# Handing out PSUM banks by age instead of by turn, from the attention stage to the third branch

## What is computed

```python
z = x @ w_in_2                                   # one wide projection, cut into parts
# branch 1: differential attention, 4 heads, causal, with a position bias
a  = softmax(q1 k1^T * d**-0.5 - slope*dist) - lam * softmax(q2 k2^T * d**-0.5 - slope*dist)
oa = rms_norm(a @ v)
# branches 2 and 3: gated linear attention, state S_t = diag(exp(g_t)) S_{t-1} + k_t^T v_t
ob = rms_norm(q_t S_t) * silu(gout)              # 4 heads of 64x128, two heads to a job
oc = rms_norm(q_t S_t) * silu(hout)              # 4 heads of 128x128, one head to a job
# mixing
y   = einsum('btnc,ncd->btnd', [oa, ob, oc], w_branch)
mix = einsum('btnd,btnd->btd', sigmoid(mg), y) @ w_out_2
```

## Time and profile before

| | |
|---|---|
| median of 3 runs | 2969.69 us |
| profiled execution, its own time | 2970.0 us |
| its span, first to last instruction | 2968.0 us |
| TensorE (PE) busy | 2869.4 us, 97% |
| VectorE (DVE) busy | 1823.4 us, 61% |
| ScalarE (ACT) busy | 1134.8 us, 38% |
| GpSimd (POOL) busy | 1373.5 us, 46% |
| mean granted TensorE clock | 0.993 |
| stretch from the attention stage to the third branch | about 1117 to 2054 us of the span |
| mixing stage (`pe_branches`) | 2054 to 2228 us |

### The profile page before, as it was taken

How to read it: one execution, slowest core, us unless ns; L and a number is a source line. 1 busy time by engine, 2 the same in 40 slices (tenths; PEclk the granted TensorE clock), 3 DMA queues, 4 the chain that set the end, 5 groups by cost and what they waited for, 6 DMA issues and landing times.

```text
span 2968.0 us, 36400 instructions
## 1 busy us (share of the span) xinstructions
PE 2869.4 (97%) x14022; PEld 2361.3 (80%) x14022; DVE 1823.4 (61%) x2849; ACT 1134.8 (38%) x1649; POOL 1373.5 (46%) x697
## 2 busy tenths in 40 slices
PE   8999999999989999999999999999999999999998
PEld 7777778888878877777777887888888788888886
DVE  8837675555458775554647755652354756657886
ACT  4223354444433334344434533432231543433331
POOL 4434348977758662111211111111222599847874
PEclk9999999999999999999999999999999999999999
DMA  6342302333244321111101111124322144463441
GB/s 218 83 124 75 107 15 89 108 106 107 96 170 171 106 87 65 56 58 57 43 29 51 50 57 38 49 71 149 135 100 107 36 146 156 156 216 128 149 149 71
DMA packets 114301, 295.79 MB, mean 100 GB/s; under 512 B 14545, under 2 KB 23169, under 8 KB 114113
## 3 DMA queue, kind: packets, MB, share of 16 engines
q1 hardware_dynamic: 114128, 293.46, 29.8%
HBM read 216.61 MB, written 76.81 MB: 99 GB/s over the span
## 4 chain that ended last, share of the span: by engine, by line
PE 87%; DVE 4%; ACT 3%; POOL 3%; issue 3%; DMA 1%; SPq 0%; ACTq 0%; DVEq 0%; POOLq 0%
PE PS L493 28%; PE PS L926 23%; PE PS L1085 4%; PE PS L1083 4%; PE PS L1084 4%; PE PS L1332 3%; PE PS L533 2%; PE PS L535 2%; PE PS L534 2%; PE PS L1208 1%; POOL WL L3151 1%; PE PS L1238 1%; PE PS L559 1%; PE PS L1105 1%; PE PS L1104 1%
## 5 line engine op out<-in xcount | busy, mean ns | idle before, releaser
L3151 POOL TENSOR_TENSOR WL<-WR,WH 128x1024 fp32r<-128x1024 f32 x236 | 580.1, 2462 | 1212.2 <-ACT WH L1453 1212.0
L1453 ACT ACTIVATE WH<-WR 128x1024 fp32r<-128x1024 f32 x237 | 248.6, 1054 | 279.2 <-POOL WR L3191 137.1
L493 PE MATMUL PS<-XH,WH 128*128 128x512 f32 x1040 | 338.8, 407 | 16.2 <-DVE XL L2213 9.1
L493 PE MATMUL PS<-XL,WH 128*128 128x512 f32 x1040 | 323.0, 392 | 0.0
L493 PE MATMUL PS<-XH,WL 128*128 128x512 f32 x1040 | 321.9, 391 | 0.0
L926 PE MATMUL PS<-XH,WH 128*128 128x512 f32 x624 | 244.1, 391 | 1.6 <-ACT PC L1753 1.6
L926 PE MATMUL PS<-XL,WH 128*128 128x512 f32 x624 | 243.3, 390 | 0.0
L926 PE MATMUL PS<-XH,WL 128*128 128x512 f32 x624 | 243.2, 390 | 0.0
L2735 DVE TENSOR_TENSOR XF<-XF,PS 128x512 f32<-128x512 f32 x280 | 186.8, 682 | 77.7 <-PE PS L1085 77.5
L493 PEld LDWEIGHTS PS<-XH,WH 128*128 128x128 f32 x1040 | 183.1, 189 | 63.2 <-issue 25.1
L493 PEld LDWEIGHTS PS<-XH,WL 128*128 128x128 f32 x1040 | 195.8, 188 | 42.9
(11 more groups left out here) (407 smaller groups left out, 6119.2 us busy)
## 6 DMA issues: line engine op xcount, KB each, us to landing
WR<-in_weights SPq DMA_DIRECT2D x201, 512.0 KB, 3.6
HR<-hsum SPq DMA_DIRECT2D x70, 512.0 KB, 3.7
hsum<-CT SPq DMA_DIRECT2D x40, 512.0 KB, 3.1
DW<-in_weights SPq DMA_DIRECT2D x40, 512.0 KB, 5.4
hsum<-CT SPq DMA_DIRECT2D x40, 256.0 KB, 2.4
gates<-EG SPq DMA_DIRECT2D x18, 512.0 KB, 5.2
EI<-gates SPq DMA_DIRECT2D x18, 512.0 KB, 5.2
hbuf<-CT SPq DMA_DIRECT2D x14, 512.0 KB, 3.0
```

What stands on the lines that cost most here:

```text
L493: last = e.matmul(PS[:, u.b + h, :], w, x[:, k, 512 * h:512 * h + 512], start=k == 0 and w is w1 and x is xh, stop=k == nk - 1 and w is w2)
L1453: e.activation(WH[:, v % NSPL, :], raw_at(r), ACT.Copy).then_inc(w_hi, 1)
L3151: e.tensor_tensor(WL[:, v % NSPL, :], raw_at(r), WH[:, v % NSPL, :].bitcast(F), ALU.subtract).then_inc(w_lo, 1)
```

## The change

`Banks` gets a flag `oldest_first`, a count of events, and for each bank the number of its last event. An event is a `take` or a `let`. With the flag set, `take` without a fixed bank picks, of the banks or pairs with nothing held, the one whose last event is longest ago; of a pair the younger bank counts. The flag is set after the three opening features of the attention stage and cleared after the mixing stage, where `turn` is set to the oldest pair. Nothing else differs: neither the order of instructions on any engine, nor the data that they move, apart from the bank numbers and the semaphores that go with them.

```diff
+        self.oldest_first, self.uses, self.last_use = False, 0, [0] * 8
+
+    def mark(self, b, n):
+        self.uses += 1
+        for x in range(b, b + n):
+            self.last_use[x] = self.uses
+
+    def oldest(self, n):
+
+        free = [b for b in range(0, 8, n) if not any(x in self.held for x in range(b, b + n))]
+        return min(free, key=lambda b: max(self.last_use[b:b + n]))
 
     def take(self, name, n=1, hold=False, told=True, at=None):
-        b = -(-self.turn // n) * n % 8 if at is None else at
-        while any(x in self.held for x in range(b, b + n)):
-            b = (b + n) % 8
-        if at is None:
-            self.turn = b + n
+        if at is None and self.oldest_first:
+            b = self.oldest(n)
+        else:
+            b = -(-self.turn // n) * n % 8 if at is None else at
+            while any(x in self.held for x in range(b, b + n)):
+                b = (b + n) % 8
+            if at is None:
+                self.turn = b + n
+        self.mark(b, n)
...
     def let(self, u):
         for x in range(u.b, u.b + u.n):
             self.held.discard(x)
+        self.mark(u.b, u.n)
...
             pe_open(e, [(("dq", 0), "w_in_2", 0), (("dk", 0), "w_in_2", 512), ((("dv", 0), "x"), "w_in_2", 1024)])
+            bk.oldest_first = True
             fill = iter(())
...
             pe_branches(e)
+            bk.oldest_first = False
+            bk.turn = bk.oldest(2)
             pe_project_out(e, "x3", "w_out_2", range(4), lambda j: [(m_lo, 2 * j + 2)])
```

## The result

| | before | after |
|---|---|---|
| median of 4 runs | 2969.7 us (2967.0 to 2973.18) | 2948.45 us (2946.78 to 2948.72) |
| ratio, 95% interval | | 0.9924 [0.9911, 0.9936] |
| profiled execution, its own time | 2970.0 us | 2948.72 us |
| its span | 2968.0 us | 2946.7 us |
| mean granted clock | 0.993 | 0.992 |

The kernel is 21.25 us faster; 2950.2 (2946.0 to 2957.5) was forecast. The page after shows work of the same size. GpSimd stands before its weight cuts for 20.4 us less, as PE's slots come free that much earlier. Source lines have moved: L493 is now L509, L559 is L575, L1208 is L1224, L1221 is L1237, L1332 is L1349, L1342 is L1359, L1359 is L1376, L1382 is L1399, L2805 is L2824, L3006 is L3025, L3151 is L3170.

A forecast was written before the change was run, and what follows sets the result against it. PE, busy 97%, was taken as the bound. Gains of 16.5 + 2.7 + 1.2 less 0.85 made 19.5 us off the profiled 2970.0, so 2950.5; 0.3 lower for the median, 2950.2 us. Range 2946 to 2957.5.

The forecast's parts named there:

- The whole waits: Between 1117 and 2054 us, 16 PE waits for undrained banks vanish: 16.5 us idle, plus 2.7 us of overlaps.
- the overlap of 0.17: Without a wait, the next matmul starts 0.17 us before the modelled end of the last; each whole wait returns this.
- Waits in part: Two waits before five transposes, behind a values readout, move to the turning of VX: gain 1.2 us, not 2.3.
- New waits: Three places get a bank drained late: scores of step 28, second output lots of jobs 0 and 1; 0.85 us lost.
- Job 1: Level scores behind LG: PE gains 0.7 and DVE comes forward with it; gain taken whole, 0.9 kept for the range.
- The clock: The clock dip behind two waits in job 3, costing some 1.7 us, stays: one dip before and one after.
- the clock rival: Dips in the stretch change: the one goes, 2948.5 us (chance 0.06), or jobs 2 and 4 get it too, 2953.6 (0.05).
- Behind the stretch: After 2054 us the mixing stage and the rest keep their banks and only start earlier; loss put at nothing.
- the opening of the mixing stage: The branch operand stored and loaded again from job 5's last output transposes starts from PE; loss put at nothing.
- runs into the next engine: PE comes early but waits longer for DVE or ACT; 10.0 us lost up to job 1's levels, 2960; chance 0.10.
- slower: Attention steps of 5 to 8 key blocks: PE waits for an AT copy before each score lot; 26 us, 2976; chance 0.03.
- no effect: The waits have a second cause behind the bank, such as weights or operands; 2967 us; chance 0.04.

The follow-up runs named there:

- the tested kernel: Full change with GpSimd's low parts of weight units 180 and 181, cut in job 1, made on 8 of 1024 columns only; one run, 2945.84 us.
- the two halves: Against before: age rule in the attention stage alone, 2965.18 us (ratio 0.9978); age rule in gated and mixing stages alone, 2954.68 us (0.9943).

## Why the prediction was right, and where it was wrong

- **The whole waits: right.** 19.01 measured against 19.2, all sixteen. What carried it was to ask at each wait which lot had the new bank and when that was drained. The putting back of three gates shows cause and size by itself.
- **The cost of one wait: 0.1 too small.** To the idle time and the overlap of 0.17 comes a slower second matmul. It shows at some of the sixteen (0.10 or 0.11 before four projection steps, 0.08 before level scores, nothing before the scores of the attention), 0.8 us in all.
- **Waits in part: right.** 1.08 against 1.2, with L575 <- VX at 11 waits and 10.5 us as said.
- **New waits: right in place, a little high in size.** Measured 0.37 (AT), 0.12 and 0.46 (the two output lots), less what PE caught up: 0.57 against 0.85.
- **Job 1: the step that failed.** I wrote that L3006 at 1593.24 (2.89) stood for ACT's exponentials, that PE leads this chain, and so took the gain of 0.7 whole. In truth it stood beside a weight cut of GpSimd. The trace of before had shown it, had I asked GpSimd's timeline:

```profile
1592.10 1.23 DVE L2894 SCALAR_TENSOR_TENSOR US<-US 128x1024 f32<-128x1024 f32 x1
...
1592.53 3.05 POOL L3151 TENSOR_TENSOR WL<-WR,WH 128x1024 fp32r<-128x1024 f32 x1 [12.60 <-ACT WH L1453]
```

  The cut ends at 1595.58, and L3006 at 1593.24 + 2.89 = 1596.13, 0.55 behind it, while ACT's exponentials of 1593.77 had ended at 1594.45. That this cut was the cause in before as well is not tested there; it is the same pattern as in the tested kernel. In before L2894 came ahead of the cut and ran at 1.23; in after the same instruction (L2913) starts 0.36 behind the start of the cut and takes 3.30. So DVE is no earlier by as much as PE is: level 4 of job 1 waits 0.64 longer and takes back most of the 0.76 won 22 us before. The 0.9 that I kept for the range covers it. The Trainium skill (SBUF — State Buffer, "SBUF: two separate sides") says that the port pair shared by VectorE and GpSimd is an exclusive lock, taken also by a VectorE instruction with two inputs in SBUF against a GpSimd one that reads SBUF, and that the loser blocks until the other is done. The traces agree: the 2.89 and the 3.30 end 0.55 and 1.09 behind the cut's end, each its own usual length (0.68 and 1.23) less 0.13 to 0.14, and with a short cut the same instruction takes 1.23.
- **The clock: left as it was, and it moved.** The dip in job 3 is gone, 1.6 us, which the clock rival had put at 1.7 with a chance of 0.06. Its own total, 2948.5, is by chance the measured one. That fewer idles of PE make fewer dips is what the Trainium skill's page on the clock gate would have (TensorE: Matmul & The Clock Gate, "A second HAM failure mode: psum-queue depth-cycling"). The traces go that way in part: the two profiles with the turn rule in job 3 have one dip in the stretch each, the kernel with age counted from the take, which has more and longer waits than before, has two, and the seven others have none. But the dip of before stood behind waits of 1.17 and 0.87 that after keeps without a dip, and one of the three longest waits with age counted from the take has none behind it. So what made it go isn't settled: it may be the distance between particular waits, or where the stretch falls in time.
- **Behind the stretch: right.** The mixing stage is 176 us of solid PE as before, and the rest behind it is 900.0 to 900.7 us in all the profiles.
- **Put at nothing: the opening of the mixing stage.** The step into it (start to start of two matmuls) measures 1323 ns before, 925 and 844 in the two profiles of the changed kernel, and between 705 and 1707 in the others. It ends with the chain of the branch operand, which is stored and loaded again. The store and the first load take, from issue to landing, 5.89 + 5.98 = 11.87 us before and 5.83 + 5.64 = 11.47 after, 11.28 where the step is 705 and 12.29 where it is 1707. In all ten profiles the step is this sum less 10.5 to 10.6 us. So the 0.4 that I had put at nothing is the time of two transfers, which also differs between the two profiles of one kernel; it is no effect of the banks that anything here shows.
- **Left open.** The 1.3 us of small differences in the stretch aren't assigned, nor is what made the dip go.

The rivals: *runs into the next engine* fell by the sum of the two halves; *slower* by the single AT wait of 0.30 in 32 lots; *no effect* by the result. A relative of *slower* is real, though: with age counted from the take, the rule costs 9.9 us.

## What to carry to other kernels

When an accumulator bank is held while others rotate past it, a plain turn counter comes to it just when it is let go and its readout has only begun; hand banks out by the time of their last event, and count the release as an event. Where PE is the bound, add up its waits one by one, at their idle time plus the lost overlap and the slower second matmul (here 1.44 us for a row of 1.17), and ask of each whether it is for a bank or for data: the first goes with another bank, the second with other work put in between. Before putting the length of an instruction down to a wait for one engine, lay every engine's timeline beside it.

## What was unexpected of the hardware

- VectorE stands still beside GpSimd's weight cuts. In each of the two profiles, before and after, 78 VectorE instructions take over 1.5 us more than the usual time of their line and form (its lower quartile), and all 78 overlap an elementwise instruction of GpSimd in time; of all VectorE instructions 42% do. In before, 77 of the 78 end behind that GpSimd instruction's end by their own usual length less 0.12 to 0.24 us. Not every one stalls: of 537 such GpSimd instructions in before during which a VectorE one starts, 106 have one that is over 1 us too long. The profile books this as busy time, not as idle, so the waits of DVE don't show it; only the length against that of the same form does (3.30 against 1.23).
- A small GpSimd instruction (8 columns) takes 0.39 us in the record at one place and 0.75 at another, where it starts at the same time as a VectorE one of 0.68; neither pair showed a delay on VectorE (0.69 and 0.68).
- A stop of PE costs more than its idle time: before a projection step, 1.34 us at the first matmul and 0.10 at the second for a bracket of 1.17.
